# First attention and indexer of a two-block transformer kernel: rows of 384 score columns in place of 512

## The chip, the cores and the metric

The kernel runs on one core of a Trainium2 chip. Its time is the device time of one execution, in microseconds. A core has TensorE (PE in the profile; PEld are its weight loads), VectorE (DVE), ScalarE (ACT), GpSimd (POOL) and SyncE (SP), which here issues transfers. SBUF holds 128 partitions; TensorE writes eight PSUM banks of 128 x 512 fp32.

## The reference

The input is one sequence of 256 tokens of width 1024. Two blocks of two layers each follow one another: a sparse attention, a stick-breaking attention, then a Fourier and neighbourhood mixer, memory attentions, a gated convolution and two feed-forward networks. The change is in the first layer alone:

```python
def dsa_mixer(x, w_in, w_out, cos, sin):
    q, k, v, g, qi, wi, ki = jnp.split(x @ w_in, cuts, axis=-1)
    ...
    def block(args):
        qb, qib, wib, pb = args
        q_chunk = pb // CHUNK                      # CHUNK = 64, Q_BLOCK = 128
        rel = jax.nn.relu(jnp.einsum('bqhd,bsd->bqhs', qib, ki) * IDX_DIM ** -0.5)
        score = jnp.einsum('bqhs,bqh->bqs', rel, wib)          # 8 indexer heads
        adm = key_chunk[None, :] <= q_chunk[:, None]
        score = jnp.where(adm[None], score, -jnp.inf)
        _, idx = lax.top_k(score, k_top)                       # k_top = 64
        ...
        logits = jnp.where(sel_ok[:, None], logits, -jnp.inf)  # 16 heads of 64
        p = jax.nn.softmax(logits, axis=-1)
        return jnp.einsum('bhqk,bqkhd->bqhd', p, vs)
    ...
    return (o * jax.nn.silu(g)) @ w_out
```

A query may see keys of its own chunk of 64 and of earlier chunks. So queries 0 to 127 see only keys 0 to 127, and queries 128 to 255 may see all 256.

## The kernel before

The engines run five hand-written programs that meet at semaphores; there is no scheduler. Activations lie transposed, feature on the partition and token on the column. The weights come in 150 chunks of 1024 x 256, 1 MB each, through four buffers `raw`. For each half of a chunk ScalarE writes a rounded copy (`hi`, L718) and VectorE the rest (`lo`, L1142); TensorE then forms each product from three passes, high by high, high by low and low by high (`project`, L361). `schedule()` lists the phases in their order: the indexer's queries `qi` and key `ki`, then `qa`, `ka`, `ga` and `va` (queries, keys, gate and values of the first attention), `attA`, its output `oa`, and so on. ScalarE or VectorE empties a finished pair of banks, as the phase says.

Between `qa` and `ka` stands the indexer. For each of its 8 heads TensorE makes two products of 128 queries by 256 keys into one bank (L543), ScalarE applies ReLU to the 512 columns (L844), and VectorE adds them, times a weight per query, onto `score`, one half after the other (L1301). The two halves, query tiles t = 0 and 1, lie side by side as `[P, 2, S]`. The first head adds onto `adm`, the table that is 0 for keys that a query may see and -1e30 elsewhere. TensorE is at most two heads ahead of ReLU, and ReLU two heads ahead of the addition. Eight picks follow, one between the two weight splits of each chunk of `ga` and `va`: MAX8 finds a row's eight greatest scores (L1308) and MATCH_REPLACE8 marks them (L1309). After the eighth, L1325 makes the mask `selneg` from the marks, 0 where a key was picked and -1e30 elsewhere.

The attention has 16 heads. For head a:

- TensorE, `scores`: two products, 128 queries by 256 keys each, fp32, into bank 4 or 5 (L467)
- VectorE, `logits`: per half one instruction that adds the mask and takes the row minimum of the negative (L1232)
- ScalarE, `exponentials`: per half one Exp with its sum (L796)
- VectorE, `normalise`: reciprocal (L1240) and per half a multiplication (L1243)
- TensorE, `turn`: four transposes of 128 x 128 into bank 6 or 7 (L483), keys onto the partitions
- ScalarE: one copy of the 512 turned columns (L810)
- TensorE, `values`: for each of the two tiles of keys one product of 256 query columns, the second accumulating (L494)
- every second head VectorE multiplies by the gate (L1263), ScalarE writes the high part (L821), GpSimd the low one (L1604).

In step t TensorE's program has scores(t), turn(t - 2), values(t - 3). VectorE's has logits(t), normalise(t - 1), the gate. ScalarE's has the copy of head t - 2, the exponentials of head t, the high part. The scores of heads 0 and 1 stand inside `va`. The same helpers `logits`, `exponentials`, `normalise` and `soft_attention` serve the neighbourhood attention N and the memory attentions X0 and X1, which take 256 keys in both halves; for X the table `adm` has been overwritten with zeros.

The second attention, B, is another code and is not touched. It already leaves out the keys that the first 128 queries don't see: L581 is a product of 256 columns, L582 one of 128, L597 to L600 are four products of 128 columns for running sums, and L609 to L611 are three value products of 128 columns.

## Time and profile before

| | us |
|---|---|
| median of 3 runs | 1088.21 |
| lowest, highest | 1086.91, 1091.32 |
| span of the profiled execution | 1090.5 |
| TensorE busy in it | 1050.6 |
| VectorE, ScalarE, GpSimd busy | 700.0, 539.2, 226.2 |

The indexer stands from about 60 to 77 us of the span, `ka` to 100, `ga` and the picks to 129, `va` to 153, the attention's steps to 191, and `oa` follows. A row of instructions merges neighbours of one line: its start, its time, engine, line, operation, what it writes and reads, the form and the count; in brackets how long the engine had been idle and what released it. An fp32 product of TensorE shows as two instructions, its two passes, and a transpose as one. TensorE's instructions overlap, so the distance between two starts tells more than a duration.

### The profile page before, as it was taken

Reading aid. Unit: us, or ns where it says so; the run is one execution under the profiler, and the core shown is the slowest. Engines: PE = TensorE matmul, PEld = TensorE weight load, DVE = VectorE, ACT = ScalarE, POOL = GpSimd, SP = SyncE. Lnnn points to the kernel's source line nnn. Section 1 sums busy time; section 2 is a strip of 40 time slices with the busy share of each in tenths; the row PEclk is TensorE's granted clock in tenths of the full one; section 3 lists DMA queues with packets and bytes.
Section 4 is the critical chain, followed back from the end, with each engine's and each line's share of the span. In section 5 each row is a group of like instructions: output and inputs, shape, how many; then the busy total and the mean of one; then the engine's idle time right before and its main releaser. Section 6 shows DMA issues by size and latency. Waiting matters only on the chain.

```text
span 1090.5 us, 19954 instructions
## 1 busy us (share of the span) xinstructions
PE 1050.6 (96%) x8160; PEld 1012.0 (93%) x8160; DVE 700.0 (64%) x1002; ACT 539.2 (49%) x822; POOL 226.2 (21%) x167
## 2 busy tenths in 40 slices
PE   8969999999999999999999999999999999999996
PEld 8969986999998899979999999999999999999996
DVE  5989976674446567635555657845566655657843
ACT  4335556355548636445435436644345545436641
POOL 3745201220003423000100202521015100202520
PEclk9889999999999999999999999989999999999998
DMA  9334530646542153624452545446545452545431
GB/s 344 114 117 151 194 116 1 232 154 231 189 161 76 65 192 118 245 102 155 172 174 79 194 158 189 154 166 254 198 171 201 173 188 80 193 159 188 154 116 39
DMA packets 26624, 173.28 MB, mean 159 GB/s; under 512 B 2880, under 2 KB 5184, under 8 KB 5952
## 3 DMA queue, kind: packets, MB, share of 16 engines
q1 hardware_dynamic: 24832, 161.26, 41.4%
q10 hardware_dynamic: 1728, 11.14, 2.6%
q8 instruction: 44, 0.72, 0.3%
q14 instruction: 20, 0.16, 0.0%
HBM read 167.15 MB, written 5.24 MB: 158 GB/s over the span
## 4 chain that ended last, share of the span: by engine, by line
PE 76%; DVE 11%; ACT 5%; POOL 2%; issue 2%; DMA 1%; SPq 0%; POOLq 0%; DVEq 0%; ACTq 0%
PE bank L361 64%; DVE wl L1142 4%; PE bank L467 3%; PE bank L494 2%; DVE work L1453 2%; ACT wh L718 2%; DVE work L1172 2%; DMA vec<-vecs 1%; POOL acc L1579 1%; PE bank L483 1%; DVE work L1456 1%; PE bank L429 1%; PE bank L581 1%; ACT work L1063 1%; PE bank L645 1%
## 5 line engine op out<-in xcount | busy, mean ns | idle before, releaser
L1142 DVE TENSOR_TENSOR wl<-raw,wh 128x1024 fp32r<-128x1024 f32 x300 | 394.6, 1323 | 250.8 <-ACT wh L718 248.9
L718 ACT ACTIVATE wh<-raw 128x1024 fp32r<-128x1024 f32 x300 | 312.9, 1054 | 307.1 <-PE bank L361 289.5
L361 PE MATMUL bank<-xh,wh 128*128 128x256 f32 x1312 | 368.5, 288 | 7.7 <-DVE wl L1142 5.7
L361 PE MATMUL bank<-xh,wl 128*128 128x256 f32 x1312 | 363.8, 284 | 0.0
L361 PE MATMUL bank<-xl,wh 128*128 128x256 f32 x1312 | 340.0, 284 | 0.0
L361 PEld LDWEIGHTS bank<-xh,wh 128*128 128x128 f32 x1312 | 253.2, 193 | 9.1 <-DVE wl L1142 8.1
L361 PEld LDWEIGHTS bank<-xh,wl 128*128 128x128 f32 x1312 | 253.3, 193 | 0.2
L361 PEld LDWEIGHTS bank<-xl,wh 128*128 128x128 f32 x1312 | 238.7, 193 | 0.1
L361 PE MATMUL bank<-yh,wh 128*128 128x256 f32 x768 | 212.3, 289 | 0.9 <-ACT yh L1067 0.9
L361 PE MATMUL bank<-yh,wl 128*128 128x256 f32 x768 | 210.1, 286 | 0.0
L361 PE MATMUL bank<-yl,wh 128*128 128x256 f32 x768 | 180.8, 286 | 4.2 <-POOL yl L1614 4.2
L361 PEld LDWEIGHTS bank<-yh,wh 128*128 128x128 f32 x768 | 150.1, 195 | 2.0 <-ACT yh L1067 1.3
L361 PEld LDWEIGHTS bank<-yh,wl 128*128 128x128 f32 x768 | 150.2, 196 | 0.2
L361 PEld LDWEIGHTS bank<-yl,wh 128*128 128x128 f32 x768 | 132.3, 195 | 4.7 <-POOL yl L1614 4.7
L1610 POOL TENSOR_TENSOR work<-work,qz 128x512 f32<-128x512 f32 x20 | 31.4, 1569 | 142.6 <-ACT work L1063 140.9
L361 PE MATMUL bank<-wh,xh 128*128 128x256 f32 x192 | 54.9, 289 | 1.1 <-issue 0.8
L1579 POOL TENSOR_TENSOR acc<-work 128x512 f32<-128x512 f32 x10 | 15.8, 1580 | 190.6 <-ACT work L749 190.5
L361 PE MATMUL bank<-wl,xh 128*128 128x256 f32 x192 | 53.8, 283 | 0.0
L361 PE MATMUL bank<-wh,xl 128*128 128x256 f32 x192 | 52.4, 283 | 0.0
L1172 DVE TENSOR_TENSOR work<-work,cs 32x512 f32<-32x512 f32 (+1 forms) x44 | 44.2, 1005 | 4.1 <-DMA vec<-vecs 2.1
L1579 POOL TENSOR_TENSOR acc<-acc,work 128x512 f32<-128x512 f32 x19 | 30.4, 1598 | 69.0 <-ACT work L749 68.8
L757 ACT ACTIVATE xh<-h,vec 128x256 fp32r<-128x256 f32 x48 | 21.8, 502 | 42.2 <-DVE h L1217 42.1
(154 smaller groups left out, 1320.8 us busy)
## 6 DMA issues: line engine op xcount, KB each, us to landing
raw<-w SPq DMA_DIRECT2D x149, 1024.0 KB, 4.8
k_scratch<-kt ACTq DMA_DIRECT2D x2, 1024.0 KB, 7.2
kt<-k_scratch ACTq DMA_DIRECT2D x2, 1024.0 KB, 6.3
cs<-cst SPq DMA_DIRECT2D x1, 1152.0 KB, 13.0
raw<-w SPq DMA_DIRECT2D x2, 512.0 KB, 5.8
h<-xt SPq DMA_DIRECT2D x1, 1024.0 KB, 6.1
v<-memt ACTq DMA_DIRECT2D x1, 1024.0 KB, 8.3
m_scratch<-yh ACTq DMA_DIRECT2D x1, 1024.0 KB, 4.3
```

What stands on the lines that cost most here:

```text
L361: return pe.matmul(b[:, j, :], lhs, rhs, start=k0 + k == 0 and q == 0 and (j == 0 or not both_open), stop=k0 + k == KT * p.deep - 1 and q ...
L429: mm = pe.matmul(bank[4][:, t:t + 1], part[:, t * P:t * P + P], ones[:, 0:1], start=(e == 0), stop=(e == len(parts) - 1))
L467: mm = pe.matmul(b3(4 + a % 2)[:, t, :], l, r, start=(j == 0), stop=(j == len(ops) - 1))
L483: mm = pe.transpose(b3(6 + a % 2)[:, s, t * P:t * P + P], pr[:, t, s * P:s * P + P], ident)
L494: mm = pe.matmul(o, v[:, s, sl], wk3(4 + a % 2)[:, s, :], start=(s == 0), stop=(s == 1))
L718: act.activation(wh[:, n % 2, :, part], raw[:, n % RAW_SLOTS, :, part], ACT.Copy).then_inc(hi_ready, 1)
L757: ins = act.activation(xh[:, m, :], h[:, m, :], ACT.Copy, scale=vc(gain, m))
L1142: dve.tensor_tensor(wl[:, n % 2, :, part], raw[:, n % RAW_SLOTS, :, part], wh[:, n % 2, :, part].bitcast(F32), ALU.subtract).then_inc(lo_r ...
L1172: ins = dve.tensor_tensor(wk(4 + r % 2)[to, 0:width].rearrange("p (a b) -> p a b", a=n), wk(r % 2)[frm, 0:width].rearrange("p (a b) -> p a ...
L1453: both(*[dve.scalar_tensor_tensor(cv[:, j, :], cp[:, j, 0:S], vc(taps, 2 * c + j), cv[:, j, :], ALU.mult, ALU.add) for j in range(2)])
L1579: pool.tensor_tensor(acc[:, :, :], a, source(c), ALU.add).then_inc(acc_done, 1)
L1610: pool.tensor_tensor(wk3(7 + c % 2), a, b, ALU.mult).then_inc(pf_ready, 1)
```

## The change

The two halves of a row of scores no longer have 256 columns each. In the indexer and in attention A the first query tile takes columns 0 to 127 (keys 0 to 127) and the second 128 to 383 (all 256 keys). `NEAR` holds these two slices, `FULL` the old ones; `rows(name)` gives `NEAR` for A. Per indexer head one of two products is half as wide, as is one of two additions; ReLU covers 384 columns. In a pick one MAX8 and one MATCH_REPLACE8 of two are half as wide. Per attention head one of two score products, one of two logits, exponentials and multiplications are half as wide; three transposes stand in place of four (keys 128 to 255 of the first query tile don't exist); the copy covers 384 columns; the value product with the second tile of keys covers only the query columns 128 to 255. No instruction changes its place, no wait and no transfer is added or taken away. The scratch columns 384 to 511 stay unused.

```diff
+        zeros = c_("adm")
...
-        score, selneg = wk3(8), wk3(9)
+        FULL = (slice(0, S), slice(S, 2 * S))
+        NEAR = (slice(0, P), slice(P, P + S))
+        score, selneg = wk(8), wk(9)
+
+        def rows(name):
+            return NEAR if name == "A" else FULL
...
-                        ops = [(qz[:, a, part], kt[:, a // 2, :])]
+                        ops = [(qz[:, a, part], kt[:, a // 2, 0:S if t else P])]
...
-                        mm = pe.matmul(b3(4 + a % 2)[:, t, :], l, r, start=(j == 0), stop=(j == len(ops) - 1))
+                        mm = pe.matmul(bank[4 + a % 2][:, rows(name)[t]], l, r, start=(j == 0), stop=(j == len(ops) - 1))
...
-                        for t in range(2):
-                            mm = pe.transpose(b3(6 + a % 2)[:, s, t * P:t * P + P], pr[:, t, s * P:s * P + P], ident)
+                        for t in range(s if near else 0, 2):
+
+                            at = 2 * P * s + P * (t - s if near else t)
+                            key = rows(name)[t].start + P * s
+                            mm = pe.transpose(bank[6 + a % 2][:, at:at + P], pr[:, key:key + P], ident)
...
-                        for s in range(2):
-                            mm = pe.matmul(o, v[:, s, sl], wk3(4 + a % 2)[:, s, :], start=(s == 0), stop=(s == 1))
+                        pe.matmul(o, v[:, 0, sl], wk(4 + a % 2)[:, 0:S], start=True, stop=False)
+                        late = slice(P, S) if name == "A" else slice(0, S)
+                        mm = pe.matmul(o[:, late], v[:, 1, sl], wk(4 + a % 2)[:, S:S + late.stop - late.start],
+                                       start=False, stop=True)
...
-                    mm = pe.matmul(b3(4 + a % 2)[:, t, :], qiz[:, a, t * P:t * P + P], ki, start=True, stop=True)
+                    mm = pe.matmul(bank[4 + a % 2][:, NEAR[t]], qiz[:, a, t * P:t * P + P], ki[:, 0:S if t else P],
+                                   start=True, stop=True)
...
-                    act.activation(wk3((2, 3, 6)[t % 3])[:, q, :], wk3(t % 2)[:, q, :], ACT.Exp,
+                    act.activation(wk((2, 3, 6)[t % 3])[:, rows(name)[q]], wk(t % 2)[:, rows(name)[q]], ACT.Exp,
...
-                        act.activation(wk(4 + a % 2), bank[6 + a % 2][:, :], ACT.Copy).then_inc(t_evac, 1)
+                        turned = 3 * P if name == "A" else 4 * P
+                        act.activation(wk(4 + a % 2)[:, 0:turned], bank[6 + a % 2][:, 0:turned], ACT.Copy).then_inc(t_evac, 1)
...
-                act.activation(wk(6 + a % 2), bank[4 + a % 2][:, :], ACT.Relu, scale=HD ** -0.5).then_inc(rel_ready, 1)
+                act.activation(wk(6 + a % 2)[:, 0:P + S], bank[4 + a % 2][:, 0:P + S], ACT.Relu,
+                               scale=HD ** -0.5).then_inc(rel_ready, 1)
...
-                    dve.tensor_tensor_reduce(wk3(t % 2)[:, q, :], b3(4 + t % 2)[:, q, :], bias[:, q, :],
+                    at = rows(name)[q]
+                    dve.tensor_tensor_reduce(wk(t % 2)[:, at], bank[4 + t % 2][:, at], bias[:, at],
...
-                    dve.tensor_scalar(pr[:, q, :], pr[:, q, :], erec[:, u, q:q + 1], None, ALU.mult).then_inc(p_ready, 1)
+                    at = rows(name)[q]
+                    dve.tensor_scalar(pr[:, at], pr[:, at], erec[:, u, q:q + 1], None, ALU.mult).then_inc(p_ready, 1)
...
-                    dve.scalar_tensor_tensor(score[:, t, :], wk3(6 + a % 2)[:, t, :], wi[:, t, a:a + 1],
-                                             (score if a else adm)[:, t, :], ALU.mult, ALU.add).then_inc(is_added, 1)
+                    start = score[:, NEAR[t]] if a else adm[:, t, 0:S if t else P]
+                    dve.scalar_tensor_tensor(score[:, NEAR[t]], wk(6 + a % 2)[:, NEAR[t]], wi[:, t, a:a + 1],
+                                             start, ALU.mult, ALU.add).then_inc(is_added, 1)
...
-                both(*[dve.max(top8[:, t, :], score[:, t, :]) for t in range(2)])
-                both(*[dve.match_replace(score[:, t, :], top8[:, t, :], score[:, t, :], TAKEN) for t in range(2)])
+                both(*[dve.max(top8[:, t, :], score[:, NEAR[t]]) for t in range(2)])
+                both(*[dve.match_replace(score[:, NEAR[t]], top8[:, t, :], score[:, NEAR[t]], TAKEN) for t in range(2)])
...
-                    chain(dve.tensor_scalar(selneg, score, 0.5 * TAKEN, NEG, ALU.is_gt, ALU.mult))
+                    chain(dve.tensor_scalar(selneg[:, 0:P + S], score[:, 0:P + S], 0.5 * TAKEN, NEG, ALU.is_gt, ALU.mult))
```

The remaining lines give the masks of N and X a flat view (`nabias_of`, `zeros`) of the same 512 columns.

## Rows read from the trace of the kernel before

**Rows 1.** The page, parts 1 and 2: busy us, and granted clock in 40 slices.
```profile
PE 1050.6 (96%) x8160; PEld 1012.0 (93%) x8160; DVE 700.0 (64%) x1002; ACT 539.2 (49%) x822; POOL 226.2 (21%) x167
...
PEclk9889999999999999999999999989999999999998
```

**Rows 2.** The chain of waits from 157 to 163 us, its shares by line.
```profile
by line: PE bank L467 46.1%; PE bank L494 39.6%; PE bank L483 21.9%
```

**Rows 3.** TensorE in order of time, first attention: start us, us, engine, line, form.
```profile
153.25 0.66 PE L483 MATMUL bank<-cs,work 128*128 128x128 f32 x4 [0.32 <-DVE work L1243]
...
157.81 1.08 PE L494 MATMUL bank<-work,v 128*64 128x256 f32 x4
158.82 1.13 PE L467 MATMUL bank<-kt,qz 128*128 128x256 f32 x4
159.78 0.60 PE L483 MATMUL bank<-cs,work 128*128 128x128 f32 x4
160.31 1.08 PE L494 MATMUL bank<-work,v 128*64 128x256 f32 x4
```

**Rows 4.** Stretches: length, busy PE, PEld, DVE, ACT, POOL, granted clock, DMA share, GB/s.
```profile
157.44:182.49 25.05, 25.05 (x123) 16.41 (x121) 16.37 (x75) 17.27 (x55) 3.00 (x5) 1.00 0.00 1
345.73:358.44 12.71, 12.71 (x92) 10.99 (x91) 8.10 (x17) 10.67 (x25) 6.66 (x8) 1.00 0.01 2
```

**Rows 5.** TensorE in order of time, one head of the second attention.
```profile
345.73 0.70 PE L581 MATMUL bank<-qz,kt 128*128 128x256 f32 x2
346.26 0.38 PE L582 MATMUL bank<-qz,kt 128*128 128x128 f32 x2
346.48 0.39 PE L597 MATMUL bank<-work,cs 128*128 128x128 f32 x2
...
347.47 0.43 PE L609 MATMUL bank<-work,v 128*64 128x128 f32 x2
...
348.27 0.70 PE L581 MATMUL bank<-qz,kt 128*128 128x256 f32 x2
```

**Rows 6.** Groups by line, whole span and attention; then one copy of 256 columns.
```profile
L1394 DVE TENSOR_TENSOR work<-bank,cs 128x384 f32<-128x384 f32 x16 | 8.8, 548 | 0.0
...
L1232 DVE CUSTOM_DVE_ANT_0 work<-bank,work 128x256 f32<-128x256 f32 x20 | 7.7, 422 | 8.8 <-PE bank L467 8.8
...
L796 ACT ACTIVATE work<-work,nmax 128x256 f32<-128x256 f32 x20 | 9.9, 497 | 0.0
...
28.84 0.38 ACT L739 ACTIVATE work<-bank 128x256 f32<-128x256 f32 x1 [4.55 <-POOL gt L1564]
```

**Rows 7.** The indexer in order of time on VectorE, ScalarE, TensorE; then a stretch.
```profile
68.27 1.89 DVE L1301 SCALAR_TENSOR_TENSOR work<-work,wi,cs 128x256 f32<-128x256 f32 x2
...
76.88 1.75 DVE L1301 SCALAR_TENSOR_TENSOR work<-work,wi 128x256 f32<-128x256 f32 x4 [0.55 <-ACT work L844]
...
73.01 0.60 ACT L844 ACTIVATE work<-bank 128x512 f32<-128x512 f32 x1 [0.36 <-PE bank L543]
74.81 0.60 ACT L844 ACTIVATE work<-bank 128x512 f32<-128x512 f32 x1 [1.20 <-PE bank L543]
...
70.90 6.17 PE L543 MATMUL bank<-work,gt 128*128 128x256 f32 x16 [6.98 <-ACT work L844]
...
69.00:75.80 6.80, 4.90 (x11) 3.70 (x12) 5.80 (x10) 2.39 (x4) 2.20 (x2) 0.50 0.00 1
```

**Rows 8.** Waits from 104 to 116 us, and the first pick in the chain of waits.
```profile
PE bank L361 <- DVE wl L1142: 1.8, 2, 1.3
...
110.42 0.68 DVE top L1308 x2
```

**Rows 9.** VectorE and GpSimd in order of time at the attention's end.
```profile
185.93 0.62 DVE L1243 TENSOR_SCALAR work<-work,erec 128x256 f32<-128x256 f32 x2
...
187.28 1.08 DVE L1243 TENSOR_SCALAR work<-work,erec 128x256 f32<-128x256 f32 x2
...
187.43 0.79 POOL L1604 TENSOR_TENSOR yl<-work,yh 128x256 fp32r<-128x256 f32 x1 [4.28 <-ACT yh L821]
```

More of the change, by code:

```diff
@@ L232, in build, with nabias_of @@
         wiw = v[:, :, :].rearrange("p a b -> p (a b)")[:, KT * P:KT * P + KT * IH].rearrange("p (k n) -> p k n", k=KT)
+        zeros = c_("adm")
         nabias = qz[:, 4:12, :].rearrange("p (h t) s -> p h t s", t=2)
+        def nabias_of(a):
+            return nabias[:, a, :, :].rearrange("p t s -> p (t s)")
         u_tok = qz[:, 12:16, :].rearrange("p a b -> p (a b)").rearrange("p (t n) -> p t n", t=2)
@@ L479, in turn @@
                         pe.wait_ge(t_evac, u - 1)
-                    pr = wk3((2, 3, 6)[a % 3])
+                    pr = wk((2, 3, 6)[a % 3])
+                    near = name == "A"
                     for s in range(2):
-                        for t in range(2):
-                            mm = pe.transpose(b3(6 + a % 2)[:, s, t * P:t * P + P], pr[:, t, s * P:s * P + P], ident)
+                        for t in range(s if near else 0, 2):
+                            at = 2 * P * s + P * (t - s if near else t)
+                            key = rows(name)[t].start + P * s
+                            mm = pe.transpose(bank[6 + a % 2][:, at:at + P], pr[:, key:key + P], ident)
                     mm.then_inc(t_full, 1)
@@ L1240, in normalise @@
                 chain(dve.reciprocal(erec[:, u, :], esum[:, u, :]))
[L1241 removed]
+                pr = wk((2, 3, 6)[t % 3])
                 for q in range(2):
[L1243 removed]
+                    at = rows(name)[q]
+                    dve.tensor_scalar(pr[:, at], pr[:, at], erec[:, u, q:q + 1], None, ALU.mult).then_inc(p_ready, 1)
             def soft_attention(name, heads, bias, scale, extra, lag):
@@ L1438, in _ @@
             for a in range(2):
-                logits("N", a, nabias[:, a, :, :], NA_SCALE)
+                logits("N", a, nabias_of(a), NA_SCALE)
             normalise("N", 0)
@@ L1445, in _ @@
                                   ALU.subtract).then_inc(dve_evac, 1)
-            soft_attention("N", 4, lambda a: nabias[:, a, :, :], NA_SCALE, plain_low("N", 1, 4), 4)
+            soft_attention("N", 4, lambda a: nabias_of(a), NA_SCALE, plain_low("N", 1, 4), 4)
             residual("oab", "xa0", "xa0")
@@ L1506, in queries @@
                     if c == 2:
-                        logits("X" + l, 0, adm, XA_SCALE)
+                        logits("X" + l, 0, zeros, XA_SCALE)
                 def second_logits(c, l=l):
@@ L1511, in second_logits @@
                         normalise("X" + l, 0)
-                        logits("X" + l, 1, adm, XA_SCALE)
+                        logits("X" + l, 1, zeros, XA_SCALE)
                 chunks("qx" + l, queries, middle=second_logits, split=1, hold=True)
-                soft_attention("X" + l, 4, lambda a: adm, XA_SCALE, plain_low("X" + l, 2, 0), 4)
+                soft_attention("X" + l, 4, lambda a: zeros, XA_SCALE, plain_low("X" + l, 2, 0), 4)
                 residual("ox" + l, "ffn" + l, "ffn" + l)
```

1 line of the change is left out of this document (removed).

## The prediction

> **What bounds the kernel now.** I read the page first, then the order of the chain of waits in the first attention, then TensorE's own rows there, and last the stages ahead of it. TensorE is busy for 1050.6 of 1090.5 us [rows 1], so only what shortens TensorE's work, or a wait of TensorE, moves the end. In the first attention the chain runs over three lines of TensorE and nothing else: L467 (scores), L494 (values), L483 (transposes) [rows 2]. The reader should see that no ScalarE or VectorE line stands in it. TensorE's starts repeat with one head: values 157.81, scores 158.82, transposes 159.78, values again 160.31. That is 1.01 + 0.96 + 0.53 = 2.50 us a head [rows 3], and TensorE is busy for the whole 25.05 us of ten heads, at a granted clock of 1.00 [rows 4]. In the same stretch ScalarE is busy for 17.27 us, VectorE for 16.37, GpSimd for 3.00. This stage is bound by TensorE's columns.
>
> **The attention, per head.** Before, two score products and two value products of 256 columns and four transposes of 128. After, one of each product is 128 wide and there are three transposes. The second attention of the same program already has both forms side by side [rows 5]: the wide product (two passes) takes from 345.73 to 346.26, the narrow one behind it to 346.48, so wide and narrow together 0.75 us, against 0.96 for two wide: 0.21 less. Its three narrow value products (384 columns, what the new head has) take from 347.47 to 348.27, 0.80 us, against 1.01 here: 0.21 less. Four transposes are 0.53 us, of which one is 0.11 to 0.13 (a quarter of 0.44 to 0.53); I take 0.11, since part of the 0.53 is the change-over between groups. New head: 0.75 + 0.80 + 0.42 = 1.97 us, 0.53 less than 2.50. Sixteen heads: 16 x 0.53 = 8.5 us. The first two heads' scores stand inside the projection of the values, where TensorE has no gap either.
>
> What hides the rest: even if no ScalarE or VectorE instruction became shorter, ten heads ask 17.3 and 16.4 us of them, 1.73 and 1.64 a head, under 1.97 [rows 4]. The loop that could pace it runs over two heads: transposes end, copy (0.5), two exponentials (2 x 0.49), reciprocal (0.2), normalising (0.5), next but one transposes (0.4), with some 0.4 of hand-overs 3.0 us, against 2 x 1.97 = 3.9. It fits, with less slack than before. The softmax instructions do get shorter: 128 columns are 0.13 us on VectorE (548 ns for 384 from PSUM, 422 for 256) [rows 6] and 0.11 on ScalarE (0.60 us for 512, 0.38 for 256) [rows 6, 7]. They only buy slack.
>
> The ends of the stage don't get all of it. At the start TensorE waits 0.32 us for the first normalising [rows 3]. TensorE arrives 3 x 0.21 = 0.64 us earlier (three heads' scores), and the chain that it waits for (last pick, selneg, logits, exponential, normalising) shortens by 0.27 + 0.07 + 0.13 + 0.11 + 0.07 = 0.65 (the two 0.07 are set between nothing and 0.13), so that wait stays. At the second head I expect a new wait of about 0.24, since two exponentials and a normalising lie between, and TensorE now needs only 0.42 + 0.75 us to come back. At the last two heads there are no scores to fill: normalising is then late by about 0.5 in all instead of 0.3. In that place a normalising pair took 1.08 us instead of 0.62, beside a GpSimd subtraction [rows 9]. Together 0.4 lost: **8.1 us** from the attention.
>
> **The indexer.** It is reached with VectorE behind: the accumulation begins at 68.27, TensorE has been idle for 7 us, and its clock has dropped to 0.50 by the time it resumes at 70.90 [rows 7]. From there sixteen passes take 6.17 us. Successive ReLUs, each started by TensorE, stand at 73.01 and 74.81: a head costs 1.80 us at the half clock. With three quarters of the columns it is 1.35. The first accumulation, 1.89 us for its two halves beside a GpSimd add, has one half of half width, so TensorE resumes about 0.45 earlier. Then 70.45 + 1.6 + 3 x 1.35 = 76.1 against 77.07: **1.0 us**. VectorE's later accumulations (1.75 us for four, so 0.44 each) ask 0.75 a head and stay under 1.35. Bounds: the time at which the clock comes back is not set by this code. If it comes a stretch later, TensorE is slow for some more of the projection behind; the half-clock stretch here took from 69 to 75.8, 6.8 us, and half of such a stretch more costs 1.7 us. If it comes that much earlier, 1.7 more is won. So -0.7 to 2.7, and I take the middle.
>
> **Picks, mask and the rest.** Each of the eight picks has a MAX8 and a MATCH_REPLACE8 at half width, 0.13 us each, 0.27 a pick. Only the first counts: between 108 and 114 us TensorE waits 1.8 us for VectorE's weight splits [rows 8], and the first pick, 0.68 us of MAX8 in the chain, stands ahead of the split awaited. The other seven lie beside TensorE's projections. The last is in the wait above. I count **0.3 us**, bounds 0 and 0.3. The neighbourhood and memory attentions get their old shapes through new names: nothing, and no cover is needed, as their instructions are the same. No transfer, wait or queue is added or moved.
>
> **Sum.** 8.1 + 1.0 + 0.3 = 9.4 us, of the profiled execution's span of 1090.5, giving 1081.1. That execution is 2.3 us above the median of the runs, 1088.2; the difference can be one more stretch at the half clock. From the median: **1078.8 us**.
>
> **A rule that speaks against it.** The rows show narrow passes at 0.11 us each in rows that load new weights every time (346.26 to 346.48 for two) [rows 5], which is their share of the columns. The Trainium skill (TensorE: Matmul & The Clock Gate, Back-to-back issue gap) says that in a stream of weight load and matmul pairs the spacing at 128 columns is about 81 ns and not the 56 of the columns alone. By that, an estimate from the page, each of four narrow passes a head would cost 25 ns more, 1.6 us over the stage, and the result would be 1080.4. The measurement here is the nearer one, and the first sum stands.
>
> **The rivals.** (1) *The softmax loop becomes the pace.* For: slack of the loop falls from 5.0 - 3.0 to 0.9 us, and normalising is stretched by 0.46 when GpSimd's subtraction falls beside it [rows 9], which the shorter period may bring about. Against: that is one stretch in two heads. If it sets 2.2 us a head, the stage gives 16 x 0.3 = 4.8, in all 6.1: 1082. Chance 9%. (2) *Narrow passes are not cheaper*, because the weight load of 128 columns sets the spacing. Then only the transposes save, 16 x 0.11 = 1.8 us, and with picks and accumulation 2.5: 1086. Against: rows 5. Chance 2%. (3) *Slower: the clock.* With narrower work TensorE streams 1.60 of 1.97 us (0.64 + 0.32 + 0.64), 81%, where it had 2.13 of 2.50, 85%. If the granted clock fell to half in the attention, a head would be 1.60 x 2 + 0.37 = 3.57 us, and the stage 16 x 1.07 = 17 us longer instead: 1104. It decides as soon as a third of the stage runs at half clock, since then the loss (a third of 16 x 1.6 = 8.5) takes the gain. Against: the second attention, with more and smaller groups, kept 1.00 [rows 4]. The Trainium skill (same page, A second HAM failure mode) describes a kernel whose short idles between groups of matmuls made the clock oscillate; no stretch of the attentions here does. Chance 3%. (4) *The clock elsewhere.* The page shows a lowered clock in three slices ahead of the last [rows 1], two of them before 82 us, around the indexer, and one near 710 us, far behind the attention; everything behind the attention now runs 9 us earlier, and one stretch of half clock more or less is 1.7 us either way. It is in the range of my forecast.
>
> **How the numbers follow.** Forecast 86%, of which most lies between 1076 and 1082. Rival 1 9%, rival 2 2%, rival 3 3%. The range is 1075 to 1084: below, the earlier return of the clock (1.7) and one stretch less elsewhere (1.7); above, rival 1 and one stretch more. A difference of 0.5%, 5.4 us, is about what a measurement of this kernel can tell from no change: faster means under 1082.8. The forecast lies 4 us beyond it; faster 0.87, same 0.09, slower 0.04.
>
> **What would show it.** Right: score pairs starting 0.75 us ahead of the transposes, three transposes in 0.42, values 0.80, a head in 1.97; TensorE still busy throughout the ten middle heads, VectorE waiting for scores every head by about 0.5; ReLUs 1.35 apart while the clock is at 0.50. Wrong: waits of TensorE's transposes on VectorE's normalising in the middle heads (rival 1), 0.4 us between the start of a narrow pair and what follows (rival 2), a granted clock under 1.00 in the attention (rival 3). The forecast as a whole fails if a head is over 2.2 us.

## The result, and the profile after

| | median us | runs | lowest to highest |
|---|---|---|---|
| kernel before | 1089.18 | 4 | 1086.91 to 1091.32 |
| changed kernel | 1079.29 | 4 | 1078.56 to 1080.66 |
| predicted | 1078.8 | | 1075 to 1084 |

The ratio is 0.991, with a 95% interval of 0.9892 to 0.9928: faster by some 10 us. A second timing, among the experiments, gave 1079.82 and a ratio of 0.9918 (0.9899 to 0.9936). Below, a difference of under some 2 us between two kernels' times is not called one.

The profiled execution of the changed kernel has a span of 1078.9 us, against 1090.5 before. These are the two lines of its page that answer to [rows 1]. The columns are busy us and the granted clock in 40 slices.

```profile
PE 1039.4 (96%) x8144; PEld 1004.7 (93%) x8144; DVE 693.4 (64%) x1002; ACT 535.6 (50%) x822; POOL 226.1 (21%) x167
...
PEclk9979999999999999999999999999999999999998
```

TensorE is busy for 11.2 us less, with 16 matmuls fewer: the transposes, one a head. TensorE is still busy for 96% of the span and bounds the kernel.

The first attention, on TensorE in order of time (start us, us, engine, line and form, and the idle time before with its releaser). L479 is the scores, L499 the transposes, L509 and L511 the wide and the narrow value product. In the kernel before they are L467, L483 and L494, [rows 3].

```profile
151.22 0.55 PE L499 MATMUL bank<-cs,work 128*128 128x128 f32 x3 [0.31 <-DVE work L1266]
...
152.59 0.55 PE L499 MATMUL bank<-cs,work 128*128 128x128 f32 x3 [0.17 <-DVE work L1266]
...
155.84 0.92 PE L479 MATMUL bank<-kt,qz 128*128 128x128 f32 x4
156.59 0.49 PE L499 MATMUL bank<-cs,work 128*128 128x128 f32 x3
157.02 0.65 PE L509 MATMUL bank<-work,v 128*64 128x256 f32 x2
157.50 0.38 PE L511 MATMUL bank<-work,v 128*64 128x128 f32 x2
157.81 0.92 PE L479 MATMUL bank<-kt,qz 128*128 128x128 f32 x4
...
177.90 0.55 PE L499 MATMUL bank<-cs,work 128*128 128x128 f32 x3 [0.28 <-DVE work L1266]
...
179.18 0.55 PE L499 MATMUL bank<-cs,work 128*128 128x128 f32 x3
...
181.09 0.39 PE L373 MATMUL bank<-yh,wh 128*128 128x256 f32 x1
```

Read the starts, not the durations, which overlap. Scores to transposes is 156.59 - 155.84 = 0.75 us, transposes to values 0.43, values to the next scores 0.79: one head in 1.97, where it was 2.50. No row of the middle heads has a bracket, so TensorE waits for nobody there. The whole stage, from the first transposes to the first output projection, takes 181.09 - 151.22 = 29.87 us. Before it was 190.77 - 153.25 = 37.52.

The same as a row of stretches (columns as in [rows 4]):

```profile
154.60:177.50 22.90, 22.90 (x129) 15.86 (x127) 16.56 (x89) 17.60 (x62) 3.65 (x5) 1.00 0.01 1
```

TensorE is busy for all of 22.90 us, at a clock of 1.00. VectorE is busy for 16.56 us of it and ScalarE for 17.60, 72% and 77%, where [rows 4] has 65% and 69%: the slack that the prediction spoke of has shrunk but is there. VectorE's own rows show what it waits for:

```profile
156.80 0.29 DVE L1254 CUSTOM_DVE_ANT_0 work<-bank,work 128x128 f32<-128x128 f32 x1 [0.67 <-PE bank L479]
...
157.01 0.42 DVE L1254 CUSTOM_DVE_ANT_0 work<-bank,work 128x256 f32<-128x256 f32 x1
...
158.77 0.29 DVE L1254 CUSTOM_DVE_ANT_0 work<-bank,work 128x128 f32<-128x128 f32 x1 [0.33 <-PE bank L479]
```

It waits for scores at every head, by 0.67 and 0.33 us in turn (in one head of two it has the multiplication by the gate to make as well), and its narrow pass takes 0.29 us beside 0.42 for the wide one.

Where the 11.6 us of the span were won, by the same places in both traces:

| place on TensorE | before | after | ahead by | won since the row above |
|---|---|---|---|---|
| first indexer accumulation (VectorE) | 68.27 | 67.91 | 0.36 | 0.36 |
| key projection behind the indexer | 76.72 | 75.37 | 1.35 | 0.99 |
| first matmul behind the first pick | 114.16 | 112.83 | 1.33 | -0.02 |
| first transposes | 153.25 | 151.22 | 2.03 | 0.70 |
| first output projection | 190.77 | 181.09 | 9.68 | 7.65 |
| end of the span | 1090.5 | 1078.9 | 11.6 | 1.9 |

The last 1.9 us lie in code that is the same in both. There the trace of before has granted-clock records of 0.50 at 413.7 (3.4 us long) and 710.7 (6.8), and the trace of after only at 699.8 (3.4), besides two that both have, one some 50 us ahead of the end and one at the end. Where such records stand differs between executions of one kernel, as the experiments show.

### The profile page after: what moved, and what is told of

Read it like the earlier page. It is cut to its first block, busy times and chain, and to the rows that moved or that the text cites. A ratio compares the mean times of both kernels' runs of the same rounds, so it can differ in the third digit from the quotient of the medians.

```text
span 1078.9 us, 19922 instructions
## 1 busy us (share of the span) xinstructions
PE 1039.4 (96%) x8144; PEld 1004.7 (93%) x8144; DVE 693.4 (64%) x1002; ACT 535.6 (50%) x822; POOL 226.1 (21%) x167
## 4 chain that ended last, share of the span: by engine, by line
PE 75%; DVE 13%; ACT 5%; issue 2%; POOL 2%; DMA 1%; SPq 0%; POOLq 0%; DVEq 0%; ACTq 0%
PE bank L373 63%; DVE wl L1163 5%; PE bank L479 2%; DVE work L1193 2%; DVE work L1477 2%; ACT wh L737 2%; PE bank L509 1%; POOL acc L1603 1%; DMA vec<-vecs 1%; DVE work L1480 1%; PE bank L499 1%; PE bank L441 1%; PE bank L511 1%; PE bank L600 1%; ACT work L1084 1%
```

## The experiments

The runs ask three things: which engine's saving makes the attention's 8 us; whether the indexer's 1 us is the packing's or the clock's; and whether the clock's part can be had otherwise. They settle the first. "Stage" is the time from the first transposes to the first output projection, "indexer" that from the first accumulation to the key projection. Times are medians, each beside runs of the kernel before on the same chip: its median was 1087.60 beside the first four rows, 1087.60 beside the next four, and 1088.88 beside the last four. Rows of different fours are best compared by their ratios.

| kernel | time (range, runs) | ratio (95%) | head | stage | indexer |
|---|---|---|---|---|---|
| after again | 1079.82 (1076.49 to 1081.04, 6) | 0.9918 (0.9899 to 0.9936) | 1.974 | 29.87 | 6.86 |
| attention alone | 1081.15 (1079.43 to 1086.29, 6) | 0.9939 (0.9916 to 0.9962) | 1.97 | 29.86 | 7.70 |
| indexer alone | 1089.33 (1087.62 to 1092.05, 12) | 1.0012 (1.0001 to 1.0023) | 2.505 | 37.65 | 6.98 |
| wide softmax | 1082.10 (1080.08 to 1082.93, 6) | 0.9943 (0.9927 to 0.996) | 1.974 | 30.16 | 7.70 |
| wide TensorE | 1088.41 (1085.96 to 1091.8, 10) | 1.0004 (0.9989 to 1.0019) | 2.505 | 37.31 | 7.11 |
| a fourth transpose | 1082.37 (1080.28 to 1083.1, 4) | 0.9943 (0.992 to 0.9965) | 2.09 | 31.76 | 7.71 |
| after, filled | 1078.60 (1075.72 to 1082.75, 6) | 0.9923 (0.9901 to 0.9944) | 1.974 | 29.87 | 6.93 |
| before, filled | 1088.62 (1087.48 to 1091.3, 12) | 1.0007 (0.9993 to 1.0021) | 2.505 | 37.52 | 7.04 |
| before again | 1088.99 (1086.6 to 1092.42, 12) | 1.0002 (0.9985 to 1.002) | 2.505 | 37.51 | 8.91 |
| indexer alone, again | 1088.98 (1086.38 to 1093.37, 12) | 1.0002 (0.9986 to 1.0019) | 2.505 | 37.65 | 7.03 |
| filled before the down projection | 1086.45 (1084.2 to 1089.81, 12) | 0.9974 (0.9959 to 0.999) | 1.97 | 29.87 | 7.70 |
| both fills | 1086.72 (1082.03 to 1091.05, 12) | 0.9983 (0.9965 to 1.0) | 1.97 | 29.88 | 6.86 |

### The changed kernel again

No edit.

> The changed kernel once more, as the control for the three beside it. Both theories: 9 to 10 us under the kernel before, near 1079. The places of its clock stretches in the profile may differ from those of its first profile; what stays is one head in 1.97 us and the attention from the first transposes to the first pass of oa in 29.9 us.

The attention came out to the hundredth: 1.974 a head, 29.87 for the stage. The indexer took 6.86 us in place of 7.46, in the same code, and the span was 1078.3. So the attention's time is the same in both executions, and the indexer's is not.

### The attention alone

The indexer's columns, picks and mask stay at 512, and the attention's softmax reads the mask in its old places.

```diff
-                    mm = pe.matmul(bank[4 + a % 2][:, NEAR[t]], qiz[:, a, t * P:t * P + P], ki[:, 0:S if t else P],
+                    mm = pe.matmul(bank[4 + a % 2][:, FULL[t]], qiz[:, a, t * P:t * P + P], ki[:, 0:S],
...
-                    dve.tensor_tensor_reduce(wk(t % 2)[:, at], bank[4 + t % 2][:, at], bias[:, at],
+                    mask = (slice(0, P), slice(S, 2 * S))[q] if name == "A" else at
+                    dve.tensor_tensor_reduce(wk(t % 2)[:, at], bank[4 + t % 2][:, at], bias[:, mask],
```

> Only the attention is packed: the indexer, the picks and the mask have their full 512 columns again, and the mask is read at columns 0 to 127 and 256 to 511. Theory: the gain is TensorE's columns in the attention, 8.3 us (7.65 between the first transposes and oa, 0.64 in the first three heads' scores); the wait for the first transposes grows, since the last pick and the mask are wide again (0.3 us), so this kernel lies 7.9 to 8.3 us under the kernel before and 1.0 to 1.4 above the packed one. Rival, that the indexer's part carries the gain through VectorE, which is behind from 20 to 114 us: this kernel gives back 3 us or more.

The stage took 29.86 us, as in the changed kernel. The wait of the first transposes rose from 0.31 to 0.53 us, because the last pick and the mask ahead of them are wide again. The ratio of 0.9939 is 6.6 us under before, and 1.3 us above the second timing of the changed kernel, which these runs don't resolve (by the ratios it is 2.3). The attention alone has most of the gain. The expected 7.9 to 8.3 us are above the 6.6, but inside its interval (4.1 to 9.1).

### The indexer alone

The attention keeps 512 columns. The mask is spread to them by two instructions and a fill.

```diff
-                        ops = [(qz[:, a, part], kt[:, a // 2, 0:S if t else P])]
+                        ops = [(qz[:, a, part], kt[:, a // 2, :])]
...
-                    near = name == "A"
+                    near = False
```

> Only the indexer and the picks are packed; the attention has its 512 columns again, with the mask spread out by two instructions in place of one and its unused quarter filled once earlier on VectorE. Theory: 1.0 us under the kernel before, from the four indexer heads at the half clock, which a measurement of five rounds can only just see; bounds 0 and 2.7, as the clock falls. A head of the attention costs 2.50 us. Rival (the indexer carries the gain): 3 us or more.

The head is back at 2.505 us and the stage at 37.65. The indexer took 6.98 us. The first output projection starts at 188.97, against 190.77 in the trace of before, but the run time doesn't show it: 1089.33, a ratio just above 1, whose interval leaves no room for the gain of 1.0 us that was expected. A second timing below takes this up.

### A wide softmax over narrow TensorE work

TensorE does what it does in the changed kernel; VectorE and ScalarE work on 256 and 256 columns, as before, and the mask is spread to them as in the run above.

```diff
         def rows(name):
-            return NEAR if name == "A" else FULL
+            return FULL
...
-                        mm = pe.matmul(bank[4 + a % 2][:, rows(name)[t]], l, r, start=(j == 0), stop=(j == len(ops) - 1))
+                        at = slice(0, P) if name == "A" and t == 0 else rows(name)[t]
+                        mm = pe.matmul(bank[4 + a % 2][:, at], l, r, start=(j == 0), stop=(j == len(ops) - 1))
```

> TensorE's products and transposes are packed as in the changed kernel, and so are the indexer, the picks and the copy, but logits, exponentials and the multiplication of the attention have 256 columns in both halves (the extra quarter is masked). Theory (TensorE's columns set the pace, and the shorter softmax only buys slack): a head stays at 1.97 us, the waits at the two ends grow by 0.3 to 0.5, and the time is within 0.6 us of the changed kernel. Rival (the loop over softmax is close to being the pace): a head over 2.05 us, and 1.5 us or more above the changed kernel.

This is the test of the first rival, the softmax loop as the pace. TensorE's rows of this kernel, over one head (L480 scores, L500 transposes):

```profile
157.59 0.92 PE L480 MATMUL bank<-kt,qz 128*128 128x128 f32 x4
158.35 0.49 PE L500 MATMUL bank<-cs,work 128*128 128x128 f32 x3
...
159.56 0.92 PE L480 MATMUL bank<-kt,qz 128*128 128x128 f32 x4
```

159.56 - 157.59 = 1.97, and no wait. VectorE still has spare time beside it:

```profile
158.55 0.42 DVE L1255 CUSTOM_DVE_ANT_0 work<-bank,work 128x256 f32<-128x256 f32 x1 [0.47 <-PE bank L480]
...
160.52 0.42 DVE L1255 CUSTOM_DVE_ANT_0 work<-bank,work 128x256 f32<-128x256 f32 x1
```

It waits 0.47 us for scores in one head and not in the next. So even the old softmax keeps up with the new TensorE: shorter VectorE and ScalarE instructions buy slack and nothing in the middle heads. They do count at the ends, where TensorE has nothing to put in between:

```profile
152.88 0.55 PE L500 MATMUL bank<-cs,work 128*128 128x128 f32 x3 [0.68 <-DVE work L1267]
...
154.34 0.55 PE L500 MATMUL bank<-cs,work 128*128 128x128 f32 x3 [0.26 <-DVE work L1267]
...
179.85 0.55 PE L500 MATMUL bank<-cs,work 128*128 128x128 f32 x3 [0.48 <-DVE work L1267]
```

0.68, 0.26 and 0.48 where the changed kernel has 0.31, 0.17 and 0.28: 0.66 us more. The run time was 2.3 us above the second timing of the changed kernel, more than that and more than the 0.6 us that the theory allowed; the rival's 1.5 us is met, but not its head of over 2.05 us. In this trace the indexer's part took 0.84 us longer than in that one (7.70 against 6.86); what is left, under 1 us, isn't resolved.

### Wide TensorE work under a narrow softmax

Two wide score products, four transposes and two wide value products; VectorE and ScalarE on 384 columns.

```diff
-                        ops = [(qz[:, a, part], kt[:, a // 2, 0:S if t else P])]
+                        ops = [(qz[:, a, part], kt[:, a // 2, :])]
...
+                    if near:
+                        mm = pe.transpose(bank[6 + a % 2][:, 3 * P:4 * P], pr[:, 0:P], ident)
...
-                        mm = pe.matmul(o[:, late], v[:, 1, sl], wk(4 + a % 2)[:, S:S + late.stop - late.start],
+                        turned = slice(P, P + S) if name == "A" else slice(S, 2 * S)
+                        mm = pe.matmul(o, v[:, 1, sl], wk(4 + a % 2)[:, turned],
```

> The reverse of the wide softmax: logits, exponentials, multiplications, copy, indexer and picks stay packed, but TensorE gets its columns back in the attention. Both score products are 256 wide (the second overwrites what the first wrote too much), a fourth transpose goes into the unused quarter, and both value products cover 256 query columns, so the first 128 queries take in a wrong product and the output is not the reference's. Theory (TensorE's columns are the gain): a head costs 2.50 us again, the stage 37.5, and the kernel lies 8.0 to 8.6 us above the changed one, 1 to 2 under the kernel before. Rival (the shorter softmax carries part): under 7 us above the changed one, and a head under 2.4 us.

```profile
156.42 1.13 PE L480 MATMUL bank<-kt,qz 128*128 128x256 f32 x4
157.39 0.49 PE L500 MATMUL bank<-cs,work 128*128 128x128 f32 x3
157.72 0.27 PE L502 MATMUL bank<-cs,work 128*128 128x128 f32 x1
157.92 0.65 PE L512 MATMUL bank<-work,v 128*64 128x256 f32 x2
...
158.93 1.13 PE L480 MATMUL bank<-kt,qz 128*128 128x256 f32 x4
```

One head is 158.93 - 156.42 = 2.51 us, split as in [rows 3]: scores 0.97, transposes 0.53, values 1.01. The time is 1088.41, no different from before and 8.6 us above the second timing of the changed kernel (9.4 by the ratios). The 1 to 2 us under the kernel before that were expected did not show: the interval ends at 1.2. With the run before, this shows from both sides that the attention's gain is TensorE's columns, but for some 0.7 us of waits at its ends.

### A fourth transpose

The changed kernel with one transpose more a head, whose result nobody reads.

```diff
+                    if near:
+                        mm = pe.transpose(bank[6 + a % 2][:, 3 * P:4 * P], pr[:, 0:P], ident)
```

> The changed kernel with a fourth transpose of each head into the unused quarter of the bank, which nothing reads. Theory: 0.11 us a head, so a head in 2.08 us and 16 x 0.11 = 1.7 us more in all; the three other removals then hold 0.42 of the 0.53. Rival (a transpose costs a quarter of its group, 0.13): 2.11 us and 2.1 more. If a group's change-over hid it: nothing.

```profile
156.11 0.92 PE L479 MATMUL bank<-kt,qz 128*128 128x128 f32 x4
156.87 0.49 PE L499 MATMUL bank<-cs,work 128*128 128x128 f32 x3
157.20 0.27 PE L501 MATMUL bank<-cs,work 128*128 128x128 f32 x1
157.40 0.65 PE L511 MATMUL bank<-work,v 128*64 128x256 f32 x2
...
158.20 0.92 PE L479 MATMUL bank<-kt,qz 128*128 128x128 f32 x4
```

The transposes take 157.40 - 156.87 = 0.53 us instead of 0.43, and a head 2.09. Over the stage it is 31.76 - 29.87 = 1.89 us, 0.118 a head: this is halfway between the 0.11 of the prediction and the 0.13 of a plain quarter, and the run doesn't decide between them. It does show that the transpose isn't hidden by the group's change-over. The time is 2.6 us above the second timing of the changed kernel, which agrees with 1.9 within what two timings can tell.

### The changed kernel with TensorE kept busy around the indexer

12 products of ones into an unused bank ahead of the indexer, and 24 ahead of its fifth head.

```diff
+            def keep_busy(n):
+                for _ in range(n):
+                    pe.matmul(bank[7][:, 0:P], ones[:, :], ones[:, :], start=True, stop=True)
+
+            keep_busy(12)
             pe.wait_ge(rope_done, 3)
             pe.wait_ge(wi_ready, 1)
             for a in range(IH):
+                if a == 4:
+                    keep_busy(24)
```

> The changed kernel, and TensorE is kept at work while it waits for VectorE ahead of the indexer and in it: 12 products of 128 columns before the first indexer head and 24 before the fifth, into a bank that nothing reads. Theory: the granted clock stays at 1.00, the last four indexer heads cost 0.75 us each (VectorE's additions set that) in place of 1.35, TensorE leaves the indexer 1.5 to 2.5 us earlier, and the kernel lies 1 to 2 us under the changed one. Rival 1 (VectorE is the pace from there to 114 us and takes it all back): TensorE leaves earlier but waits longer ahead of ga, and the time is that of the changed kernel. Rival 2 (the clock is down when the 24 begin): they take 10 us in place of 5 and the kernel is up to 3 us slower.

The granted clock over the whole execution rose to 0.995, and the only record of 0.50 near the indexer was 3.4 us long, where the two traces of the changed kernel have two, of 13.6 and 10.2 us together. The indexer's part was 6.93 us, no less than without the filling (6.86 and 7.46 in the changed kernel's two traces). The clock did not stay up in the last four heads, as the theory had it: behind the 24 products TensorE was idle for 2.12 us once more, and the record of 0.50 begins at 69.8, 0.3 us after it resumed.

```profile
61.84 5.52 PE L557 MATMUL bank<-ones 128*128 128x128 f32 x48
69.48 1.38 PE L568 MATMUL bank<-work,gt 128*128 128x128 f32 x4 [2.12 <-ACT work L871]
```

The span was 1073.9 in the profile, the shortest of this kernel's six runs. The median of the runs was 1078.60 against 1079.82, which isn't resolved.

### The kernel before with the same filling

The same lines in the kernel before.

> The kernel before with the same 12 and 24 products. Theory: the last four indexer heads, 1.80 us each at the half clock, cost 0.96 each at the full one, 3 us less; of this the part that VectorE leaves, 2 us, arrives: 2 us under the kernel before, so that the packing of the indexer alone would be worth nothing once the clock is up. Rival: unchanged time, since VectorE sets the pace there.

What the wide indexer does with the clock at full is plain in the stretch from 66 to 76 us (columns as in [rows 4]) and in VectorE's row for the accumulations:

```profile
66.00:76.00 10.00, 7.69 (x50) 6.55 (x49) 9.74 (x18) 4.19 (x7) 2.82 (x2) 1.00 0.01 2
```

```profile
62.85 5.52 PE L539 MATMUL bank<-ones 128*128 128x128 f32 x48
...
69.19 7.12 DVE L1308 SCALAR_TENSOR_TENSOR work<-work,wi 128x256 f32<-128x256 f32 x14
```

The clock is 1.00, and VectorE runs through 14 accumulations without a gap. It has become the pace here, at 1.0 us a head (7.12 us for seven). The part took 7.04 us, 1.4 to 1.9 less than in the two unfilled traces of before (8.45, 8.91) and 0.7 less than in the attention alone (7.70), whose indexer is wide too. With the packing and a filling it is 6.93 and 6.86, though with a record of 3.4 us at the half clock in each, so there the packing is worth 0.1 to 0.2 us, close to the nothing that was expected. The run time was 1088.62: no gain to be seen.

The traces flatter this filling. Its profiled execution is the shortest of its 12 (1085.7 us of span), while the two of the kernel before are among the longer ones: of the 87 runs of that kernel beside the experiments, 25 have a span of 1088.1 or more and 11 one of 1090.5 or more.

### The kernel before, once more, and the indexer alone, once more

The kernel before and the indexer alone, side by side on one chip, since the runs above didn't agree with the traces.

> The kernel before, timed against itself. It shows what a ratio of two such sets of runs is when nothing differs, and a second profile whose clock stretches lie elsewhere. Every theory: a ratio whose interval holds 1. If its median differs from its own control by 1 us or more, differences of 1 us between the other kernels say nothing.

> The kernel with only the indexer and the picks packed, once more. Theory A (its 1.0 us in the indexer is real in the trace, but other clock stretches hide it in the times): its stretch from the first accumulation to ka is 0.5 to 1.4 us shorter than that of the kernel before beside it, and its time is within 1.5 us of it on either side. Theory B (packing the indexer is a loss of 1.5 us, as its first timing has it): 1 us or more over the kernel before again, with a place in the trace behind the indexer where it is lost.

The stretch from 66 to 76 us in the kernel before:

```profile
66.00:76.00 10.00, 5.24 (x12) 3.97 (x13) 8.93 (x16) 2.39 (x4) 2.81 (x2) 0.52 0.03 14
```

and with the indexer packed:

```profile
66.00:76.00 10.00, 5.62 (x23) 4.57 (x24) 8.85 (x18) 3.06 (x7) 2.68 (x2) 0.66 0.03 13
```

The first has 12 of TensorE's records and a clock of 0.52. The second has 23 and 0.66: TensorE is through with the indexer at 75.00, not at 77.04, and is back in the projections within the stretch. The part took 7.03 against 8.91 us. At the first output projection the packed one is still 2.2 us ahead, and its profiled span is 2.3 us shorter (1085.8 against 1088.1). The medians are equal, 1088.98 and 1088.99, with intervals of 2 us either way. The 1.7 us by which the first timing of the indexer alone was longer than its neighbours did not come back. So the packed indexer gains in each pair of traces, and in neither timing: the second neither shows nor excludes 1 us, and the first excludes it.

The granted clocks of the single runs say more. At 0.984 the ten runs of the indexer alone (both timings) have a mean of 1089.1 us, and the 13 of the kernel before beside them 1090.5; at 0.987 and 0.988 it is 1087.5 (5 runs) against 1087.9 (17). At the same clock the packed indexer is thus the faster by 0.4 to 1.4 us. But its mean clock is lower, 0.9847 over 24 runs against 0.9869 over 64, and since in those 64 a clock lower by 0.001 goes with a time longer by 0.6 us, this takes the gain back. The kernel with wide TensorE work, whose indexer is packed too, has 0.9851 against 0.9877. Whether the packing lowers the clock, or these samples differ by chance, no run here separates; the six runs of the changed kernel have 0.9867.

### Filling the other wait at half clock

Far behind the attention, in the first block's down projection, a half-clock record begins at 699.8 in the changed kernel, within a wait of TensorE of 2.12 us that ends at 700.35. Eight products of ones were to fill it.

```diff
                                 if early and j == 0:
+                                    if name[0:2] == "fd" and k0 + k == 2 * KT - 2:
+                                        for _ in range(8):
+                                            pe.matmul(bank[7][:, 0:P], ones[:, :], ones[:, :], start=True, stop=True)
                                     pe.wait_ge(*early(k0 + k)[1])
```

> The changed kernel, and in the down projection of both feed-forward networks eight products of 128 columns into an unused bank stand ahead of the wait for the last low parts, where TensorE is idle for 2.1 us and the granted clock then was 0.50 for a stretch in the profiles. Theory: the clock stays up there in most executions, each saved stretch gives 1.7 us, so 1.5 to 3.4 us under the changed kernel, near 1077. Rival: the clock falls for another reason (what comes ahead of that wait), and the time is the changed kernel's.

The edit stands in the wrong place and tells nothing of the idea:

```profile
701.34 0.63 PE L373 MATMUL bank<-yl,wh 128*128 128x256 f32 x2 [2.12 <-POOL yl L1641]
705.82 1.95 PE L395 MATMUL bank<-ones 128*128 128x128 f32 x16
...
1058.58 1.95 PE L395 MATMUL bank<-ones 128*128 128x128 f32 x16
```

The wait of 2.12 us is untouched. The products stand 4.5 us behind it, where TensorE has work of its own, and the loop passes them four times (at 730.64 and 1033.76 too). They last 4 x 1.95 = 7.8 us. From the first product of the second attention to the end the trace takes 764.7 us, where the second trace of the changed kernel, with as much half clock there, takes 757.5: 7.2 us more. The time is 6.6 us above the second timing of the changed kernel (1086.45 against 1079.82), 6.1 by the ratios. All that it teaches is that a product added to a full TensorE comes back in the trace at nearly its whole length.

> Both sets of extra products: those ahead of and in the indexer, and those in the two down projections. Theory: the gains add, 0.5 us more than with the down projections alone, near 1076.5. Rival: VectorE takes the indexer's part back, and it is equal to the kernel with the down projections' products alone.

With the same fault, 1086.72, equal to the run above. The fill around the indexer again cannot be seen in the time. A fill that stands inside the 2.12 us was not tried.

## Why the prediction was right, and where it wasn't

**The attention.** 8.1 us were forecast, and the traces have 8.3: 7.65 in the stage and 0.70 between the first pick and the stage, where the narrow scores of three heads account for 3 x 0.21 = 0.64. The terms per head, 0.75, 0.42 and 0.80, read 0.75, 0.43 and 0.79. The two costs at the ends were both a little smaller. The new wait at the second head is 0.17 us where 0.24 was worked out. The waits at the last two heads were to grow from 0.3 to 0.5 and are 0.28, all in one row; before they were 0.15 and 0.16. The wait at the first transposes stayed, 0.31 against 0.32 [rows 3], for the reason given: TensorE arrives earlier by as much as the chain that it waits for got shorter.

**The doubt at the end of the attention.** [rows 9] had a normalising of 1.08 us beside a GpSimd subtraction, and the prediction feared more of it with the shorter period. It did not come: the pair at 178.46 takes 0.55 us, though a subtraction starts beside its second half.

```profile
178.46 0.55 DVE L1266 TENSOR_SCALAR work<-work,erec 128x128 f32<-128x128 f32 x2
...
178.70 0.89 POOL L1628 TENSOR_TENSOR yl<-work,yh 128x256 fp32r<-128x256 f32 x1 [3.22 <-ACT yh L841]
```

**The indexer.** 1.0 us was forecast and 0.99 measured between these two traces. The other traces show how much of that is luck. In eight traces with the packed indexer and no filling the part took 6.86 to 7.71 us, 7.32 in the mean; in three with the wide one 7.70 to 8.91, 8.35 in the mean. The means are 1.0 apart, but a single pair could have shown nothing (7.71 against 7.70) or 2.0 (6.86 against 8.91), within the bounds of -0.7 to 2.7. Most of that scatter is the clock's, as the same traces show when they are sorted by the record of 0.50 that stands in the part:

| record of 0.50 | wide indexer | packed indexer |
|---|---|---|
| 10.2 us | 8.91 | 7.70, 7.70, 7.71 |
| 6.8 us | 8.45 | 6.86, 6.98, 7.03, 7.11, 7.46 |
| 3.4 us | 7.70 | 6.86, 6.93 (both filled) |
| none | 7.04 (filled) | no trace |

In each of the first three rows the packed indexer is the shorter, by 0.8 to 1.6 us, and the two traces that are compared here both have a record of 6.8 us. So the middle of the bounds came out because the clock fell for as long in both: that part is luck, and the gain beside equal records is not. TensorE resumed at 70.29 (70.45 forecast) and was through at 75.72 (76.1 forecast), of which 0.36 comes from ahead of the indexer. The heads at half clock came out shorter, though not evenly:

```profile
72.08 0.49 ACT L864 ACTIVATE work<-bank 128x384 f32<-128x384 f32 x1 [0.17 <-DVE work L1325]
73.65 0.49 ACT L864 ACTIVATE work<-bank 128x384 f32<-128x384 f32 x1 [1.08 <-PE bank L561]
...
74.93 0.49 ACT L864 ACTIVATE work<-bank 128x384 f32<-128x384 f32 x1 [0.79 <-DVE work L1325]
```

1.57 and 1.28 us between ReLUs, 1.43 in the mean, where 1.35 was forecast and [rows 7] has 1.80. The last one waits for VectorE by the record, no longer for TensorE, so VectorE is close to being the pace there.

**The first pick.** 0.3 us was forecast, and the trace gives nothing. The saving is there and is lost in the next instruction. The chain of waits of the changed kernel, in order of time:

```profile
107.85 1.23 DVE wl L1163
109.08 0.54 DVE top L1332 x2
...
109.72 0.68 DVE work L1333 x2
...
110.43 2.27 DVE wl L1163
```

The pick's MAX8 fell from 0.68 ([rows 8]) to 0.54 us, and its replacing pair from 0.81 to 0.68. But the weight split behind it, which TensorE waits for, rose from 1.99 to 2.27 us. In the kernel before the chain has:

```profile
111.20 0.81 DVE work L1309 x2
...
112.04 1.99 DVE wl L1142
```

What stands beside the split on GpSimd is one accumulation of the weighted sum, first after and then before:

```profile
110.31 1.30 POOL L1603 TENSOR_TENSOR acc<-work 128x512 f32<-128x512 f32 x1
```

```profile
111.65 1.29 POOL L1579 TENSOR_TENSOR acc<-work 128x512 f32<-128x512 f32 x1
```

It runs until 111.61, over 1.18 us of the split that begins at 110.43. Before, it ran until 112.94, over 0.90 of the split that began at 112.04. So the split grew by 0.28 us for 0.28 us of overlap more, and it ends 1.09 us behind the end of GpSimd's accumulation in both. This holds in all 14 traces, within 0.01 us: the split takes 1.99 to 2.00 us where the pick is wide (four traces), 2.25 to 2.27 where it is narrow (ten), and ends as far behind the accumulation. The accumulation in turn follows GpSimd's instruction before it (L1588, at 107.97 after, 109.31 before), which was started by VectorE's work ahead of the pick, so nothing in the pick can move it. In the first row above, the split of 1.23 us has L1588 beside it and is not slowed; there VectorE's instruction had begun first (107.85 against 107.97), whereas at 110.43 GpSimd's had. The step that failed is the one behind "stands ahead of the split awaited": the prediction gave the split the same length whenever it starts, and so passed the pick's 0.27 us on to TensorE. The runs show a split that ends with GpSimd's instruction, so the pick's term is -0.02 us and not 0.3. No run moved GpSimd's instruction alone.

**The rivals.** *The softmax loop as the pace* fell with the wide softmax, which keeps 1.97 us a head. *Narrow passes not cheaper* fell with the rows: scores to transposes is 0.75 us for a wide and a narrow product, where two wide ones took 0.96. *The clock in the attention* did not fall: 1.00 throughout, as in every trace here. The rule of 81 ns for a narrow pair (the Trainium skill, TensorE: Matmul & The Clock Gate, Back-to-back issue gap), by which the time would be 1080.4, does not show in these passes. The narrow products save 0.21 us in the scores and 0.22 in the values, which is two passes of 0.11 each, and with 25 ns more on each narrow pass it would be 0.05 less. A narrow fp32 pass takes 0.11 us here, longer than 81 ns, so these rows don't put the rule itself to the test. *The clock elsewhere* is the rival that lives. It gave 1.9 us between the two profiled executions, and the medians, 9.9 us apart, have little or none of it.

**The sum.** 8.1 + 1.0 + 0.3 = 9.4 against 8.3 + 1.0 + 0.0 = 9.3 by the places of the traces, 0.36 us more ahead of the indexer, in unchanged code, and 9.9 between the medians. Two small terms were off by 0.2 and 0.3 in opposite directions; that the sum is nearer than its terms is luck.

## What to carry to other kernels

When one engine is busy without a gap in a stage, price a change by that engine's starts, from one group to the same group a head later, and check the others only for slack; the forms that will be wanted often stand already in another stage of the same trace. A saving upstream of a wait counts only if everything that shares the path moves with it: an instruction on a neighbour engine that stays in place can take it back, here all of 0.27 us. What a stage gains while TensorE is at the half clock should be judged over several traces, and between traces whose half-clock records are alike. And before a trace is taken for the kernel, look where its run lies among the others: here the two traces of the kernel before were of long executions.

## What the runs showed of the hardware

The half-clock records differ from execution to execution of the same kernel. In the indexer they lasted 10.2 us in one trace of the kernel before (66.4 to 76.6) and 6.8 in the other (69.0 to 75.8); later ones appeared at 413.7 in one and at 230.2 in the other. One record of 3.4 us that falls where TensorE is full costs 1.5 us: from the first output projection to the first product of the second attention it is 138.14 to 138.16 us in the five traces without one there, and 139.64 to 139.68 in the nine with one.

A half clock can also cost nothing. In the changed kernel the first four heads of the indexer ran at it, in the order of time on TensorE:

```profile
59.77 5.35 PE L561 MATMUL bank<-work,gt 128*128 128x128 f32 x16 [4.14 <-DVE wi L1314]
```

In both traces of the kernel before, at the full clock, the same heads took 3.79 us though half of their products are wider. The first accumulation still began at 67.91, against 68.27 and 68.13, since VectorE was busy until then with something else. The mean clock of an execution therefore goes with its time only over many runs (above) and says little of one stage; there it counts which wait a slow stretch ends in.

With TensorE kept busy the granted clock was higher (1.00 instead of 0.52 in the stretch from 66 to 76 us of the kernel before; 0.9898 instead of 0.9877 in the mean over the runs), and the indexer's part was 0.7 to 1.9 us shorter than in the unfilled traces of a wide indexer. No run time showed a gain from it. That the unfilled traces are of long executions is a part of the answer; the rest is open.

A VectorE instruction that begins behind a GpSimd one can be held up by it: the weight split beside the accumulation took 1.99 to 2.27 us in place of 1.23, and ended 1.08 to 1.09 us after it in all 14 traces.
